# Prompt attention: GpSimd scales the second head group's probabilities from query tile 4 on

## The reference, cut to what matters

```python
sc = einsum('bqghd,bngd->bghqn', q, kc) * scale          # compressed keys, 63 of them
oc = einsum('bghqn,bngd->bqghd', softmax(mask(sc)), vc)
ss = einsum('bqghd,bgqsd->bghqs', q, ksel) * scale       # "selected" keys
osel = einsum('bghqs,bgqsd->bqghd', softmax(mask(ss)), vsel)
sw = einsum('bqghd,bsgd->bghqs', q, kw) * scale          # window of 512 keys
ow = einsum('bghqs,bsgd->bqghd', softmax(mask(sw)), vw)
o = gates[..., 0:1] * oc + gates[..., 1:2] * osel + gates[..., 2:3] * ow
```

## Time and profile before

| | |
|---|---|
| median of 3 runs | 2679.93 us (2677.24 to 2680.45) |
| the profiled execution, own time | 2684.05 us |
| its span in the profile | 2682.4 us |
| busy in the span: TensorE | 2548.9 us (95%) |
| busy: VectorE | 910.6 us (34%) |
| busy: ScalarE | 637.6 us (24%) |
| busy: GpSimd | 488.2 us (18%) |
| mean granted TensorE clock | 0.971 |

### The profile page before, as it was taken

The page is one execution under the profiler, slowest core; times in us unless marked ns, Lnnn a source line. Parts: engine busy times, 40 slices in busy tenths (PEclk is TensorE's granted clock), DMA queues, the critical chain, the costliest instruction groups (busy, mean ns, idle before and its releaser), DMA issues.

```text
span 2682.4 us, 44571 instructions
## 1 busy us (share of the span) xinstructions
PE 2548.9 (95%) x18150; PEld 2119.5 (79%) x18150; DVE 910.6 (34%) x2512; ACT 637.6 (24%) x1629; POOL 488.2 (18%) x477
## 2 busy tenths in 40 slices
PE   7999978989988879979999999999999999999997
PEld 3555546446655645579999999999999999999996
DVE  1133144227656433334222232232333332323222
ACT  1112132226656413311111111111111111111110
POOL 0000032010000101221232222132232322313131
PEclk9999988989999879989999999999999999999999
DMA  5000057022000252387688778889898999999997
GB/s 205 13 24 21 15 157 132 5 85 103 1 1 1 90 164 94 119 300 265 222 268 277 256 267 293 282 276 315 280 322 300 328 312 325 314 329 313 330 310 251
DMA packets 284148, 534.06 MB, mean 199 GB/s; under 512 B 53647, under 2 KB 96495, under 8 KB 283732
## 3 DMA queue, kind: packets, MB, share of 16 engines
q1 hardware_dynamic: 235732, 474.35, 49.9%
q0 software_dynamic: 33392, 47.40, 8.2%
q10 hardware_dynamic: 14816, 9.41, 1.3%
HBM read 492.74 MB, written 43.48 MB: 200 GB/s over the span
## 4 chain that ended last, share of the span: by engine, by line
PE 60%; DMA 2%; DVE 0%; POOL 0%; issue 0%; SPq 0%; ACT 0%; POOLq 0%; DVEq 0%
PE eo L2242 36%; PE eo L2268 18%; PE eo L2119 4%; PE erp L2155 1%; DMA cache_rows<-in_w_up 1%; DMA w_up<-summed_rows 1%; DMA out_xp<-cache_rows 0%; PE etp L2141 0%; POOL summed_rows L2056 0%; DMA summed_rows<-window_rows,row_index_cur 0%; DMA slot_tokens_gates<-token_gate_s,dest_s 0%; SPq L2029 0%; POOL x_rows L2050 0%; DMA x_rows<-h_rows,row_index_cur 0%; PE rankp L2177 0%
## 5 line engine op out<-in xcount | busy, mean ns | idle before, releaser
L2242 PE MATMUL eo<-rg_oret,w_up 128*128 128x128 f32 (+19 forms) x4096 | 507.0, 286 | 4.6 <-DVE rg_oret L2544 4.6
L2242 PEld LDWEIGHTS eo<-rg_oret,w_up 128*128 128x128 f32 x4096 | 503.9, 191 | 4.9 <-DVE rg_oret L2544 4.9
L2242 PE MATMUL eo<-rg_oret,cache_rows 128*128 128x128 f32 (+19 forms) x4096 | 505.3, 285 | 0.5 <-DMA cache_rows<-in_w_up 0.5
L2242 PEld LDWEIGHTS eo<-rg_oret,cache_rows 128*128 128x128 f32 x4096 | 502.1, 191 | 0.7 <-DMA cache_rows<-in_w_up 0.7
L2268 PE MATMUL eo<-rg_oret,mixT 128*128 128x128 f32 (+19 forms) x3968 | 493.2, 286 | 0.0
L2268 PEld LDWEIGHTS eo<-rg_oret,mixT 128*128 128x128 f32 x3968 | 489.2, 191 | 1.1
L2563 DVE TENSOR_SCALAR window_rows<-eo,b_up_cur 128x128 f32<-128x128 f32 (+19 forms) x256 | 93.7, 366 | 1000.4 <-PE eo L2242 1000.4
L2056 POOL DMA_INDIRECT summed_rows<-window_rows,row_index_cur x149 | 235.3, 1579 | 1056.1 <-ACT window_rows L2344 1020.2
L358 PE MATMUL zp<-w_in,xnT 128*128 128x512 f32 (+2 forms) x800 | 306.0, 539 | 1.4 <-DVE xnT L576 1.4
L2355 ACT ACTIVATE window_rows<-window_rows 128x128 f32<-128x128 f32 (+19 forms) x256 | 82.4, 322 | 853.0 <-DVE window_rows L2563 853.0
L358 PEld LDWEIGHTS zp<-w_in,xnT 128*128 128x128 f32 x800 | 146.1, 193 | 139.6 <-issue 122.8
(11 more groups left out here) (474 smaller groups left out, 2065.4 us busy)
## 6 DMA issues: line engine op xcount, KB each, us to landing
w_up<-in_w_up SPq DMA_DIRECT2D x64, 2048.0 KB
cache_rows<-in_w_up SPq DMA_DIRECT2D x64, 2048.0 KB, 13.1
mixT<-in_w_down SPq DMA_DIRECT2D x64, 2048.0 KB, 12.4
w_in<-in_w_in SPq DMA_DIRECT2D x3, 2048.0 KB, 12.5
x<-in_x_prompt SPq DMA_DIRECT2D x8, 512.0 KB, 3.8
window_rows<-in_x_prompt SPq DMA_DIRECT2D x8, 512.0 KB, 3.6
summed_rows<-window_rows SPq DMA_DIRECT2D x8, 512.0 KB, 2.7
h_rows<-h SPq DMA_DIRECT2D x8, 512.0 KB, 3.6
```

Of the source, the lines that this page charges most:

```text
L2242: mm = nc.tensor.matmul(up[c % 2][:, h, :N], U[c // 4][:, h, kk, w0:w0 + P], hT[:, kk, :N], start=(kk == 0), stop=(kk == KC - 1))
```

## The change

From query tile 4 on, for the units L and W, the two multiplications of `scale` no longer both run on VectorE. VectorE multiplies the reciprocal of the second group by its gate (one number for each partition) and signals GpSimd; VectorE then scales the first group as before and signals TensorE; GpSimd scales the second group with one multiplication and signals TensorE through a second semaphore. `turn` waits for both. VectorE also waits, before it writes a slot of `rs` again, until GpSimd is through with the unit that used it four units earlier. Tiles 0 to 3 and the units C and M stay as they are.

```diff
+        s_rs, s_p1 = sem("p_scale_ready"), sem("second_group_scaled")
+        shared = lambda x: wide(x)
+        n_shared = lambda x: sum(shared(y) for y in range(x))
...
         def _(pool):
             nc.gpsimd.memset(zero[:], 0.0).then_inc(s_z, 1)
             load_caches(pool, k, True)
+            for x in range(len(UNITS)):
+                if shared(x):
+                    kind, qt, c = UNITS[x]
+                    w, b = width(kind, qt), base(kind)
+                    p = pbuf(qt, c)[:, 1, b:b + w]
+                    pool.wait_ge(s_rs, n_shared(x) + 1)
+                    nc.gpsimd.tensor_scalar(p, p, rs[:, x % 4, 1:2], None, ALU.mult).then_inc(s_p1, 1)
...
                 pe.wait_ge(s_p, x + 1)
+                if shared(x):
+                    pe.wait_ge(s_p1, n_shared(x) + 1)
...
                 else:
+                    if x >= 4 and n_shared(x - 3):
+                        dve.wait_ge(s_p1, n_shared(x - 3))
                     link(nc.vector.reciprocal(rs[:, r, 0:G], den[:, r, 0:G]))
                     w, b = width(kind, qt), base(kind)
+                    if shared(x):
+                        gt = HPG * 3 + c * 3 + (1 if kind == "L" else 2)
+                        nc.vector.tensor_scalar(rs[:, r, 1:2], rs[:, r, 1:2], k.gate[:, qt, gt:gt + 1], None, ALU.mult).then_inc(s_rs, 1)
+                        p = pbuf(qt, c)[:, 0, b:b + w]
+                        gt = c * 3 + (1 if kind == "L" else 2)
+                        nc.vector.tensor_scalar(p, p, rs[:, r, 0:1], k.gate[:, qt, gt:gt + 1], ALU.mult, ALU.mult).then_inc(s_p, 1)
+                        return
                     for g in range(G):
```

## The result

The changed kernel takes 2697.61 us (median of 4 runs, 2695.97 to 2698.2), the kernel before 2679.75 (4 runs, 2677.24 to 2680.45). The ratio is 1.0059, with an interval of 1.0047 to 1.0071. The forecast of 2681 us and its range up to 2692 are missed; the case "GpSimd is slower than a copy" had the right side and half of the size.

A forecast was written before the change was run, and what follows sets the result against it. It took the score loop and TensorE, both full, to bound the prompt stage, with room on VectorE. Terms of -0.4, +1.4 and +0.2 gave +1.2 us on 2679.93, about 2681 us, range 2676 to 2692.

The forecast's parts named there:

- GpSimd is slower than a copy: Rival: GpSimd's multiplication runs at twice the copy's slope, +8.9 us, 2689 us; chance 0.38.
- The bound and the path: Prompt stage between barriers: its microseconds come out whole; TensorE and the score loop are full, VectorE has room.
- four places: Behind C or M units in tiles 4 to 6, where TensorE's transposes already waited for scaled data, 9.0 us in all.
- Term 1: C unit of tile 7: VectorE's saved 0.45 us shortens the loop there, -0.4 us.
- Turn-taking: Wide units: VectorE's double-rate multiplication blocks GpSimd on SBUF, so the second group is ready at 1.73 us, not 1.19.
- I take the copy's figure, since this too is one operand read and one written: GpSimd's multiplication in wide units taken at the copy's 0.84 ns a column, 0.72 us for 640 columns.
- upper bound: GpSimd's multiplication at most twice the copy's slope, 1.68 ns a column, 1.26 us for 640 columns.
- the sum: All wide units together: -0.4 + 1.4 + 0.2 = +1.2 us on the whole time.
- Terms 2 and 3: Late transposes: 4 x 0.34 = +1.4 us behind C or M units; +0.2 us at L units of tiles 5 and 6.
- In full, since TensorE has no slack: Late L units of tiles 5 and 6: their whole lateness, +0.2 us, counts as lost time.
- The clock rival: Shorter or shifted waits behind C and M units miss TensorE's four clock falls, 1.4 us each: 2673 us; chance 0.06.
- the case without turn-taking: Rival: VectorE and GpSimd work side by side, second group ready at 1.19 us, sum -1.2 us, 2679 us; chance 0.11.

The follow-up runs named there:

- e4_scale_first: Kernel before, with VectorE scaling a wide unit ahead of a following C or M unit's maxima, nothing on GpSimd: 2671.47 us against 2684.47, ratio 0.9955.
- e3_late_tiles: Changed kernel, sharing with GpSimd only the 14 of 32 wide units behind the M unit of tile 6: 2683.03 us against 2684.47, ratio 0.9997.
- e5_tt: Changed kernel, GpSimd multiplying through tensor_tensor with the factor repeated along the columns: 2687.69 us in one run, kernel before 2685.13.
- e7_both: Changed kernel, with VectorE scaling a wide unit ahead of a following C or M unit's maxima: 2684.68 us, kernel before 2685.13, ratio 0.9994.
- e2_behind: Changed kernel, GpSimd's multiplication also waiting until VectorE's of the first group is done: 2701.98 us in one run, kernel before 2684.47.
- e1_copy: Changed kernel, GpSimd copying its columns onto themselves instead of multiplying: 2684.1 us, kernel before 2684.47, ratio 0.9999.

## Why the prediction was wrong

- **The bound and the path: right.** The stage's time comes out in the whole (13.1 us of stretch and 13.0 of time in `e4_scale_first`, 15.9 and 17.9 in the changed kernel), VectorE's time was not on the path, and the regular cycles and four places are where lateness costs. `e3_late_tiles` and the unchanged intervals of tiles 6 and 7 show that it costs nothing elsewhere.
- **Term 1, -0.4 us: right.** It is in every kernel that shares the last W unit of tile 6 in VectorE's old order (0.3 us in `e5_tt`, 0.4 in the others). In `e7_both` it is absent: against `e4_scale_first` that interval does not change.
- **Turn-taking: right.** The extra of 0.29 and 0.49 us over `e2_behind` grows with VectorE's own length. The Trainium skill's rule ("SBUF — State Buffer", Who interferes with whom), that the later of the two is blocked, agrees with these. VectorE's instruction kept its 0.60 us, so it was always the one that came first; the other order was not tried.
- **The step that failed is "I take the copy's figure, since this too is one operand read and one written".** GpSimd's multiplication costs 2.50 ns a column by itself, the copy 0.84, and the "upper bound" of 1.68 was no bound: it was twice a row for another operation, and nothing in the trace limits what GpSimd's arithmetic adds. With the copy in its place (`e1_copy`) the stretch grows by 0.4 us where the sum said 1.2 (0.8 at the four places, -0.4 at the C unit of tile 7, nothing in the regular cycles), so the rest of the sum was not what failed. The sentence of the Trainium skill that argued against me ("GPSIMD Engine Reference", Engine selection: elementwise work belongs on VectorE) was right in its direction. The 1.03 and 1.8 cycles an element of the Trainium skill ("GPSIMD Engine Reference", Elementwise — side-by-side cycle accounting) are 0.86 and 1.5 ns at its 1.2 GHz, and neither is the measured 2.50.
- **Terms 2 and 3, +1.4 and +0.2 us: right in mechanism, mis-sized by that rate.** They measured 6.4 and 9.8 us. The readiness of 2.78 us gives 4 x 1.39 = 5.6 for the places; the rest is about what the longer fall of the clock costs.
- **"In full, since TensorE has no slack": too strict.** By 2.78 - 1.82 a regular unit of tile 4 would be 0.96 us late; the six regular intervals of tile 4 grow by 0.76, 0, 0.74, 0.24, 0.70 and 0.96 us. One thing in the rows that gives room: TensorE, late in one unit, begins the next scores later after the reciprocal (0.41 us at 736.75 instead of 0.11). That this explains the smaller ones is argued, not shown.
- **The clock rival** was right in its mechanism, and its 1.4 us for a fall was near the 1.6 that `e3_late_tiles` shows, but the change was the wrong lever for it; `e4_scale_first` pulled the right one. Its sum adds the 1.2 us that the case without turn-taking gains; beside the forecast's +1.2, four missed falls would have left 5.6 - 1.2 = 4.4 us.
- Open: where the 2 us lie by which the medians differ more than the stretch does (17.9 against 15.9). The two profiles do not show them: outside the stretch the changed kernel's is 2.4 us the shorter one.

## What to carry to other kernels

Before work is moved to GpSimd, its rate for that very operation and instruction form must be known; a copy's rate says nothing about arithmetic, and a doubled row is not an upper bound. Relief of an engine is worth only the places where another waits for it: here VectorE's paid at one place, behind one of 32 units. Where such a wait is found, look first at what stands in front of the awaited instruction in its queue: moving it ahead of an instruction that only waits was worth 13 us, without any second engine.

## What the runs showed of the hardware

- GpSimd, float32, 128 partitions, in SBUF: `tensor_scalar` 0.28 us + 2.50 ns a column (640 and 1024 columns, `e2_behind`); the copy 0.19 us + 0.84 ns (128 and 256 columns); a constant factor makes no difference of note (2.10 against 2.18 us at 640).
- `tensor_tensor` with a repeated operand is faster than `tensor_scalar` for the same product: 1.55 against 2.18 us at 640 columns, both beside VectorE.
- A GpSimd instruction that starts while VectorE multiplies at double rate shows the blocking inside its own duration (2.18 instead of 1.88 us), not as idle time before it.
- In the kernel before, each of the four waits of 1.98 to 2.52 us on TensorE was followed by a fall of the granted clock to its lower level. It is not certain to follow: in `e3_late_tiles` it did not come behind a wait of 2.51 us, and that interval was 1.6 us shorter. With the waits gone (`e4_scale_first`) the granted clock was 1.00 throughout.
